# Moving the Mamba half of an output projection into the recurrent rounds before it

## The chip, the cores and the metric

One core of a Trainium2 chip runs the whole program. The metric is the device time of one execution in microseconds (us). TensorE multiplies, VectorE and ScalarE read its results from PSUM (eight banks of 512 float32 columns per partition), GpSimd and SyncE help with masks and transfers. A float32 product appears in the trace as two matmul records and two weight loads.

## The reference, cut to what matters

One inference step of a hybrid trunk with one layer. 384 tokens (128 of a prompt, 256 of a sample; three tiles of 128) with 1024 channels pass a modulated norm and an input projection. Two groups of heads work side by side. The Mamba group gives `ym` (384 x 1024). The RWKV group gives `yr` (384 x 1024), from a recurrence with a matrix state per head in two directions. Then

```
mix = jnp.concatenate([ym, yr], axis=-1) @ w_out        # w_out: 2048 x 1024
x = x + (gate1 * mix).astype(x.dtype)
h = rmsnorm(x, norm2_w) * (1.0 + scale2) + shift2
x = x + (gate2 * hierarchical_moe(h, ...)).astype(x.dtype)
```

The gates are row vectors, one for the prompt and one for the sample. The product with `w_out` is a sum of two halves: `ym` with the first 1024 rows of `w_out`, and `yr` with the last 1024.

## The kernel before, in words

The stages follow one another: modulation and input projection (to 350 us), the Mamba group (to about 468 us), the RWKV group (to 904 us), the out projection (904 to 995 us), norm and router (to 1029 us) and sixteen pairs of experts with their overflow (to the end). The order of instructions on every engine is written out by hand, and engines wait for each other by semaphores that count.

`mixm` holds `ym` with channels on partitions, eight tiles of 128 x 384, from the end of the Mamba group on. The RWKV group works through eight pairs of heads, one in each round (`round_pe`, `round_act`, `round_dve`, with c from 0 to 7; round 1 is c = 0). Its results take the place of tiles 0 to 7 of `um_a`.

A round has this order on TensorE. First come the small gram products (L485, L492) and one pair of larger ones (L513). Then four levels invert triangular blocks of 32 x 32: `blocks_32` (L531) multiplies 16 blocks for each of three units, ScalarE copies each unit (L754), `blocks_32` multiplies again, and VectorE merges (L930) and transposes (L933). One more group of gram products lies in each level. Then come pair products and half inverses (L544 to L563), the joining products (L616, L624), and the right sides, solutions `u`, states and outputs `y_out` (L637 to L688) for the units.

Between them `fill` puts twelve small products of the round before and of the round to come. Their numbers are MEAN, VAR (group norm of the pair before), KSQ (squared keys, L440), W_UP and W_UP + 1, A_UP and A_UP + 1 (decays and rates, two directions, each with 64 rows, L445), V_T (transpose), G_UP (L453), BE_T and KAP_T (four transposes each, L457) and BONUS. `aux_bank` puts even numbers in PSUM bank 6 and odd ones in bank 7, and `aux_free` lets a product start when the product two before it has been read:

```
def aux_bank(n, width):
    return ps[:, 6 + n % 2, 0:width]
...
pe.wait_ge(aux_act, c * 10 + (10 + n - 2))
```

ScalarE reads BE_T and KAP_T (L722, L724) at the very end of its round, behind `u_copy(2)` (L789). Before that come the exponentials, `y_copy(0)`, `rhs_copy(2)` and `y_copy(1)`.

SyncE's queue in the rounds holds only three loads of 64 KB a round, the next up projections. Once round 7 has released the space it loads 2 MB of `w_out`, and after the last round 6 MB more into the ring (`ring_a`), and the input `x` again.

The out projection (L1756 to L1777) has four blocks of four rows of tiles, 24 products of 512 columns each: two blocks with `mixm` and two with `um_a`. All sum up in PSUM banks 0 to 5 (three tiles, two halves of 512 columns). `gate_rows` (L1113) spreads a gate vector over the partitions in banks 6 and 7, and ScalarE copies it (L1999). VectorE then multiplies each tile of the product by the gate and adds it to `x` (L2313, L2315) in `x1_tile`.

Of the kernel before, what the change touches and what calls it, by code (L numbers as in the profile page):

```python
# [102 lines left out]
def program(nc, a, out):  # L103
    ctx = ExitStack()
    with ctx:
# [94 lines left out]
        us = [at(r, 3840, 2, 2, 64) for r in ring_s]  # L200
        sg = at(misc, 0, 2, T)
# [42 lines left out]
        vec_t = sem("vectors_transposed")  # L244
# [6 lines left out]
        cond_T = sem("conditions_transposed")  # L251
        ident_ok = sem("identity_ready")
        sel32_ok = sem("selector_ready")
# [144 lines left out]
        def aux_bank(n, width):  # L398
            return ps[:, 6 + n % 2, 0:width]

        def aux_free(pe, c, n):

            if n == MEAN:
                pe.wait_ge(aux_act, c * 10 + 10)
            elif n == VAR:
                pe.wait_ge(aux_dve, c * 2 + 2)
            elif n == KSQ:
# [3 lines left out]
            return aux_bank(n, T)  # L411
# [23 lines left out]
        def prep_pe(pe, c, n):  # L435
# [18 lines left out]
            elif n < BONUS:  # L454
                pe.wait_ge(ab_ok, c * 2 + (n - BE_T + 3))
                for i, (d, j) in enumerate(UNITS):
                    mm = pe.transpose(aux_bank(n, 4 * P)[:, P * i:P * i + P], (be, kap)[n - BE_T][:, d, j, :], ident[:, :])  # L457
# [108 lines left out]

        def round_pe(pe, c, b, prev, nxt):
# [132 lines left out]
            y_out(1)  # L700
            u(2)
            fill(BE_T, KAP_T)
# [3 lines left out]
        def prep_act(act, c, b, n):  # L706

            aux_there(act, c, n)
            src = aux_bank(n, T)
# [11 lines left out]
            elif n == BE_T:  # L721
                ins = act.activation(btks[b].rearrange("p i t -> p (i t)"), aux_bank(n, 4 * P), ACT.Copy)  # L722
            else:
                ins = act.activation(ktks[b].rearrange("p i t -> p (i t)"), aux_bank(n, 4 * P), ACT.Copy)  # L724
# [18 lines left out]
        def tail_act(act, c, n):  # L743
            aux_there(act, c, n)
            act.activation(ysq_c, aux_bank(n, T), ACT.Ln, scale=1.0 / 64, bias=eps_gn[:, 0:1]).then_inc(aux_act, 1)

        def round_act(act, c, b, prev, nxt):
# [3 lines left out]
            for l in range(1, 5):  # L751
# [3 lines left out]
                if l == 1:  # L755
                    if prev:
                        tail_act(act, c, VAR)
                    if nxt:
                        prep_act(act, c, 1 - b, KSQ)
                elif l == 2:  # L760
                    inverse_roots(act, c, prev, nxt)
                if nxt and l in (2, 3):
                    for n in ((W_UP, W_UP + 1) if l == 2 else (A_UP, A_UP + 1)):
# [72 lines left out]
        def prep_dve(dve, c, b, lc, part):  # L836
# [27 lines left out]
            else:  # L864
# [10 lines left out]
                dve.tensor_tensor(vbs[b], aux_bank(BONUS, T), v_c, ALU.mult).then_inc(aux_dve, 1)  # L875

        def tail_dve(dve, c, n, p, b, lc, part):

            if part == 0:
                aux_there(dve, c, n)  # L880
                dve.scalar_tensor_tensor(yc0, aux_bank(n, T), -1.0 / 64, y_c, ALU.mult, ALU.add).then_inc(aux_dve, 1)
# [214 lines left out]
        def wout_block(q):  # L1096

            if q == 0:
                return at(um_f, 8 * T, 4, D)
            return ring[:, q - 1].rearrange("p k c -> p (k c)").rearrange("p (k c) -> p k c", k=4)  # L1100

        def wout_ready(eng, q):
            if q == 0:
                eng.wait_ge(wout0_in, 16)
            else:
                eng.wait_ge(w_in_slot[q - 1], 16 * (N_BLOCKS // RING + 1))
# [150 lines left out]
        def _(sp):  # L1257
# [34 lines left out]
            with sp.Fori(0, 7) as c:  # L1292
                sp.wait_ge(aux_ps, c * 12 + 9)
                for i, w in enumerate(ups):
                    sp.dma_start(stw[:, i, :], w[:, ds(c * P + P, P)]).then_inc(up_loaded, 16)

            w_out_q = [a["w_out"][0, BLK * q:BLK * (q + 1)].rearrange("(k p) c -> p k c", p=P) for q in range(4)]
            sp.wait_ge(v_ok, 8)
            sp.wait_ge(ab_ok, 16)
            sp.dma_start(wout_block(0), w_out_q[0]).then_inc(wout0_in, 16)  # L1300
            sp.wait_ge(yo_rd, 27)
            x_row = [(x1[:, 0, :], a["x_prompt"][0]),
                     (x1[:, 1:3, :], a["x_sample"][0].rearrange("(j p) c -> p j c", p=P))]
            for q in range(1, 4):
                sp.dma_start(wout_block(q), w_out_q[q]).then_inc(w_in_slot[q - 1], 16)
# [7 lines left out]
            sp.wait_ge(out_ps, 6)  # L1313
# [48 lines left out]
        def _(pool):  # L1362
# [6 lines left out]
            pool.nop().then_inc(ident_ok, 1)  # L1369
# [37 lines left out]
            pool.wait_ge(vec_t, 1)  # L1407
# [86 lines left out]
        def _(pe):  # L1494
            pe.wait_ge(ident_ok, 1)
            pe.wait_ge(s_cond, 32)
            pe.transpose(ps[:, 0, 0:16], crows[:, :], ident[0:16, 0:16]).then_inc(cond_T, 1)
# [26 lines left out]
            pe.wait_ge(sel32_ok, 1)  # L1524
# [231 lines left out]
            for q in range(4):  # L1756
                if q == 1:
                    pe.wait_ge(pair_ok, 9)
                if q:
                    gate_rows(pe, q - 1)  # L1760
                if q == 3:
                    gate_rows(pe, 3)
                wout_ready(pe, q)
                w = wout_block(q)

                steps = ([(k, j) for k in range(4) for j in range(NTILE)] if q < 3 else
                         [(k, j) for j in range(NTILE) for k in range(4)])
# [713 lines left out]
```

## Time and profile before

| what | us |
|---|---|
| median of 3 runs | 1341.92 (1341.85 to 1343.03) |
| profiled execution, its own time | 1345.54 |
| its span, first to last instruction | 1343.8 |
| TensorE matmul busy in the span | 1178.0 (88%) |
| mean granted TensorE clock | 0.916 |
| rounds 2 to 7 | 545 to 848 |
| out projection | 904 to 995 |

Times in the rows are us from the start of the span. A busy time of TensorE means that matmuls were in flight; ends of matmuls are modelled. The granted clock is 1.0 at 2.4 GHz and 0.5 at 1.2 GHz. "issue" stands for time in which an engine waited for nothing that the profile shows.

### The profile page before, as it was taken

What the parts mean: (1) busy time and instruction counts of PE and PEld (TensorE: products, weight loads), DVE (VectorE), ACT (ScalarE), POOL (GpSimd) and SP (SyncE); (2) the same over time, 40 slices, a digit from 0 to 9 for tenths busy, and PEclk for the clock granted to TensorE, in tenths of its full rate; (3) what the DMA queues carried; (4) which work ended last, traced back from release to release, by engine and by line L of the source; (5) the groups of instructions that cost most, each with busy time, mean ns of one, the idle gap of its engine ahead of it and who ended that gap; (6) DMA issues with size and microseconds to landing.
All of it is one profiled execution on the core that took longest, in us unless ns stands there. A gap on an engine that the chain in (4) does not pass through costs nothing.

```text
span 1343.8 us, 35314 instructions
## 1 busy us (share of the span) xinstructions
PE 1178.0 (88%) x15632; PEld 780.4 (58%) x15632; DVE 576.5 (43%) x1366; ACT 336.6 (25%) x696; POOL 138.3 (10%) x186
## 2 busy tenths in 40 slices
PE   5898899999767878898888898889999999999991
PEld 4554356555566656676676676674556555555541
DVE  1354004445587565665665665530045222222214
ACT  2122011111212654444444544330012000000012
POOL 6000000000131033112022022000000000000002
PEclk9899998999877997887887987889999999999996
DMA  9436553146200000000000000115027799999974
GB/s 337 158 127 220 199 184 143 66 132 71 73 12 0 1 8 9 4 9 10 4 10 10 4 10 4 66 63 190 0 92 305 305 416 416 415 416 416 380 298 156
DMA packets 77774, 192.83 MB, mean 144 GB/s; under 512 B 11716, under 2 KB 26311, under 8 KB 73031
## 3 DMA queue, kind: packets, MB, share of 16 engines
q1 hardware_dynamic: 73504, 178.58, 36.5%
q10 hardware_dynamic: 3271, 9.08, 1.7%
q0 software_dynamic: 864, 3.15, 0.7%
q8 instruction: 113, 1.85, 0.6%
q14 instruction: 22, 0.18, 0.0%
HBM read 175.58 MB, written 15.20 MB: 142 GB/s over the span
## 4 chain that ended last, share of the span: by engine, by line
PE 78%; DVE 8%; issue 7%; ACT 3%; DMA 3%; POOL 0%; DVEq 0%; POOLq 0%; SPq 0%; ACTq 0%
PE ps L1547 15%; PE ps L1158 9%; PE ps L1147 7%; PE ps L1772 6%; PE ps L1178 5%; PE ps L531 4%; PE ps L1590 3%; PE ps L563 2%; PE ps L513 1%; DVE misc L2233 1%; DMA ring_a<-in_w_in 1%; PE ps L416 1%; PE ps L521 1%; PE ps L1509 1%; PE ps L637 1%
## 5 line engine op out<-in xcount | busy, mean ns | idle before, releaser
L1547 PE MATMUL ps<-hT,ring_a 128*128 128x384 f32 x624 | 208.3, 496 | 2.5 <-DVE hT L2087 2.5
L1547 PEld LDWEIGHTS ps<-hT,ring_a 128*128 128x128 f32 x624 | 120.2, 194 | 86.4 <-issue 5.9
L531 PE MATMUL ps<-ring_a 32*32 32x32 f32 x6144 | 74.7, 200 | 38.2 <-issue 38.1
L1147 PE MATMUL ps<-scratch,misc 128*128 128x128 f32 x864 | 99.7, 276 | 1.3 <-DVE scratch L1194 1.3
L1147 PEld LDWEIGHTS ps<-scratch,misc 128*128 128x128 f32 x864 | 97.9, 192 | 3.1 <-issue 3.1
L531 PEld LDWEIGHTS ps<-ring_a 32*32 32x32 f32 x6144 | 66.5, 112 | 56.8 <-issue 50.8
L2165 DVE SCALAR_TENSOR_TENSOR um_a<-ps,mum,um_a 128x127 f32 (+3 forms) x162 | 67.3, 416 | 71.2 <-ACT um_a L1919 42.4
L1158 PE MATMUL ps<-ring_a,um_a 128*64 128x512 f32 x288 | 63.4, 593 | 1.4 <-DVE um_a L1201 1.4
L1416 POOL TENSOR_TENSOR hT<-tri,la 128x512 f32<-128x512 f32 x24 | 25.4, 1087 | 365.6 <-PEq L1624 327.0
L1213 DVE COPY um_a<-ps 128x256 f32<-128x256 f32 x17 | 7.2, 424 | 125.5 <-PE ps L1167 125.5
L1158 PE MATMUL ps<-misc,um_a 128*64 128x512 f32 x128 | 56.3, 593 | 1.4 <-DVE um_a L1201 1.4
L1225 ACT ACTIVATE um_a<-ps 128x1024 f32<-128x1024 f32 x17 | 17.4, 1023 | 143.0 <-PE ps L1178 143.0
L1590 PE MATMUL ps<-ring_a,hT 128*128 128x512 f32 x96 | 46.8, 648 | 7.0 <-DMA ring_a<-in_w_in 7.0
L1201 DVE COPY um_a<-ps 128x1024 f32<-128x1024 f32 x17 | 20.8, 1224 | 71.4 <-PE ps L1147 70.7
L416 PE MATMUL ps<-ident 128*128 128x128 f32 x362 | 46.1, 289 | 1.6 <-DVE mixm L2286 1.6
L1488 POOL DMA_INDIRECT um_a<-expert_rows,wdt x6 | 6.7, 1121 | 395.9 <-DMA expert_rows<-um_a 390.0
L416 PEld LDWEIGHTS ps<-ident 128*128 128x128 f32 x362 | 45.4, 206 | 3.5 <-issue 2.9
L1158 PEld LDWEIGHTS ps<-ring_a,um_a 128*64 128x64 f32 x288 | 21.4, 137 | 41.3 <-issue 41.3
L930 DVE COPY_PREDICATED ring_a<-lvl,ps 128x128 f32<-128x128 int32 x96 | 26.8, 279 | 40.6 <-PE ps L531 40.5
L1772 PE MATMUL ps<-ring_a,um_a 128*128 128x512 f32 x96 | 41.5, 593 | 0.0
L1919 ACT ACTIVATE um_a<-ps,mum 128x384 f32 x24 | 13.9, 580 | 110.1 <-PE ps L1547 110.1
L2233 DVE SCALAR_TENSOR_TENSOR misc<-misc,dt,ring_a 128x128 f32<-128x128 f32 x96 | 36.0, 445 | 8.8 <-ACT misc L1943 8.8
(419 smaller groups left out, 2031.1 us busy)
## 6 DMA issues: line engine op xcount, KB each, us to landing
ring_a<-in_w_ada SPq DMA_DIRECT2D x12, 2048.0 KB, 12.6
ring_a<-in_w_in SPq DMA_DIRECT2D x11, 2048.0 KB, 9.3
ring_a<-in_moe_w_gate SPq DMA_DIRECT2D x18, 1024.0 KB, 9.6
ring_a<-in_moe_w_up SPq DMA_DIRECT2D x18, 1024.0 KB, 11.7
ring_a<-in_moe_w_down SPq DMA_DIRECT2D x18, 1024.0 KB, 11.7
expert_rows<-um_a ACTq DMA_DIRECT2D x17, 512.0 KB, 7.1
misc<-in_moe_w_gate SPq DMA_DIRECT2D x16, 512.0 KB, 9.3
misc<-in_moe_w_up SPq DMA_DIRECT2D x16, 512.0 KB, 11.8
```

The lines of the kernel that those rows point to most:

```text
L416: pe.matmul(place, ident[:, :], ident[:, :], start=True, stop=True)
L531: mm = pe.matmul(ps[r, 2 * s + 1, m:m + 32], lhs[r, h, d, :], rhs[r, h, d, :], start=True, stop=True, tile_position=(32 * q, 32 * q), skip ...
L563: mm = pe.matmul(ps[z, 2 * s + q % 2, o:o + 32], merge_of(s, d, h)[r], xcT[s][r, h, d, :], start=True, stop=True, tile_position=(32 * q, 6 ...
L930: dve.copy_predicated(xc[s], level_mask(l, False), ps[:, 2 * s + 1, P:2 * P].rearrange("p (h d q) -> p h d q", h=2, d=2)).then_inc(x_ok, 1)
L1147: mm = pe.matmul(ps[:, k // 4, P * (k % 4):P * (k % 4) + P], h2[:, j, P * k:P * k + P], pick[:, j, :], start=(j == 0), stop=(j == NTILE - 1))
L1158: mm = pe.matmul(ps[h, 2 + b, :], xgT[:, b, k, h], gate_up_tile(b, x, k), start=(k == 0), stop=(k == KT - 1), tile_position=(0, CH * x), s ...
L1178: mm = pe.matmul(ps[h, 5 + c, :], hidT[:, b, k, h], wdn[b][x][:, k, BLK * c:BLK * c + BLK], start=(k == 0), stop=(k == 1), tile_position=( ...
L1547: mm = pe.matmul(ps[:, t % 4 if isinstance(t, int) else t, 0:T], slot(n)[:, k, P * c:P * c + P], hT[:, k, :], start=(k == 0), stop=(k == K ...
L1590: mm = pe.matmul(ps[:, i % 4, :], hT[:, k, P * j:P * j + P], slot(n)[:, k, :], start=(k == 0), stop=(k == KT - 1))
L1772: mm = pe.matmul(ps[:, 2 * j + c, :], src[:, P * j:P * j + P], w[:, k, BLK * c:BLK * c + BLK], start=(kk_ == 0), stop=(kk_ == 15))
L2165: step(dve.scalar_tensor_tensor(dst, src, mus(m), dst, ALU.mult, ALU.add), i)
L2233: ins = dve.scalar_tensor_tensor(seg[:, j, 4 * d + h, :], seg[:, j, 4 * d + h, :], dt[:, j, ds(grp * 8 + (16 * d + 4 * q + h), 1)], msc[:, ...
```

## The change

The 48 products of the Mamba half are computed in rounds 2 to 7 (c from 1 to 6), eight in each: one behind the first and one behind the second group of level products of each of the four levels (`mamba_out`). A round makes one block of the half product, one tile of 128 tokens by 512 columns, and accumulates it in PSUM bank 7 over the eight channel tiles. ScalarE copies the finished block to SBUF (`half_mix`) behind V_T. For this bank 7 is taken from the small products: in the rounds all of them use bank 6, and each waits until the one before it has been read. W_UP and W_UP + 1, and A_UP and A_UP + 1, which stood together, are put in different places of the levels, KSQ moves from level 1 to level 2, and BE_T moves ahead of `u(2)`.

The weights come in 48 loads of 256 KB on SyncE's queue, three ahead, into free columns of the three ring slots. Behind the rounds only the RWKV half is left: 48 products, with the four gate products in between. Its weights come in four loads, three of them during the last rounds. VectorE multiplies the six blocks by the gate and adds them to `x` (twelve operations of 128 x 512) before `x1_tile(0)`. Three semaphores at the start are merged into others.

```diff
+        mamba_w = [at(r, 3072, BLK) for r in ring_s]
+        half_mix = [at(um_flat, (8 * T, 16 * T)[r // 3] + BLK * (r % 3), BLK) for r in range(6)]
...
-        def aux_bank(n, width):
-            return ps[:, 6 + n % 2, 0:width]
+        def aux_bank(c, n, width):
+            return ps[:, 6 + n % 2 if c < 0 or (c == 7 and n >= KSQ) else 6, 0:width]
...
-                pe.wait_ge(aux_act, c * 10 + (10 + n - 2))
+                pe.wait_ge(aux_act, c * 10 + (10 + n - 1))
...
+        def mamba_out(pe, c, k):
+
+            if not 1 <= c <= 6:
+                return
+            r, n = c - 1, 8 * (c - 1) + k
+            if k == 0 and r:
+                pe.wait_ge(half_rd, r)
+            mamba_block(pe, n)
+            pe.matmul(ps[:, 7, :], mixm[:, k, P * (r // 2):P * (r // 2) + P], mamba_w[n % RING],
+                      start=(k == 0), stop=(k == KT - 1)).then_inc(half_ps, 1)
...
                     blocks_32(pe, s, 0, diag(s), xc[s]).then_inc(yl_ps, 1)
+                mamba_out(pe, c, 2 * l - 2)
+                if l > 1:
+                    fill({2: KSQ, 3: W_UP + 1, 4: A_UP + 1}[l])
                 if l == 4:
                     gram_pair(pe, c, arr, 4)
...
                     blocks_32(pe, s, P, xcT[s], yc[s]).then_inc(zl_ps, 1)
-                if l > 1:
-                    fill(*{2: (W_UP, W_UP + 1), 3: (A_UP, A_UP + 1), 4: ()}[l])
+                mamba_out(pe, c, 2 * l - 1)
+                if l in (2, 3):
+                    fill({2: W_UP, 3: A_UP}[l])
                 if l < 4:
                     gram_pair(pe, c, arr, l)
                 if l == 1:
-                    fill(VAR, KSQ)
+                    fill(VAR)
...
             y_out(1)
+            fill(BE_T)
             u(2)
-            fill(BE_T, KAP_T)
+            fill(KAP_T)
             y_out(2)
             fill(BONUS)
...
                 prep_act(act, c, 1 - b, V_T)
+            if 1 <= c <= 6:
+                act.wait_ge(half_ps, 8 * c)
+                act.activation(half_mix[c - 1], ps[:, 7, :], ACT.Copy).then_inc(half_rd, 1)
...
+            def mamba_weights(n):
+
+                if n >= RING:
+                    sp.wait_ge(half_ps, n - RING + 1)
+                r, k = n // KT, n % KT
+                sp.dma_start(mamba_w[n % RING], a["w_out"][0, P * k:P * k + P, BLK * (r % 2):BLK * (r % 2) + BLK]
+                             ).then_inc(w_in_slot[n % RING], 16)
...
-            for q in range(4):
...
+            steps = [(k, j) for k in range(4) for j in range(NTILE)] + [(k, j) for j in range(NTILE) for k in range(4, 8)]
+            for k, j in steps:
+                if j == 0:
+                    wout_ready(pe, k)
+                    if 3 <= k < 7:
+                        if k == 3:
+                            pe.wait_ge(pair_ok, 9)
+                        gate_rows(pe, k - 3)
+                for c in range(2):
+                    mm = pe.matmul(ps[:, 2 * j + c, :], um_a[:, k, P * j:P * j + P], wout_tile(k)[:, BLK * c:BLK * c + BLK],
+                                   start=(k == 0), stop=(k == KT - 1))
+                if k == KT - 1:
                     mm.then_inc(out_ps, 1)
...
+            for r in range(6):
+                j, c = r // 2, slice(BLK * (r % 2), BLK * (r % 2) + BLK)
+                dve.tensor_tensor(half_mix[r], half_mix[r], g1[:, min(j, 1), c], ALU.mult).then_inc(half_w, 1)
+            for r in range(6):
+                j, c = r // 2, slice(BLK * (r % 2), BLK * (r % 2) + BLK)
+                dve.wait_ge(half_w, r + 1)
+                dve.tensor_tensor(x1[:, j, c], x1[:, j, c], half_mix[r], ALU.add).then_inc(half_w, 1)
+            dve.wait_ge(half_w, 12)
             x1_tile(0)
```

## Rows read from the trace of the kernel before

**Rows 1.** Chain that ended last, 900 to 1000 us: start, us, what

```profile
904.12 20.87 PE ps L1772 x48
924.98 1.78 PE ps L1113 x16
926.77 20.60 PE ps L1772 x48
...
971.58 1.03 ACT misc L1999
...
995.31 4.80 PE ps L416 x43
```

**Rows 2.** Windows of rounds 2 to 7 and of the out projection

```profile
core 0: us, PE busy (x) PEld busy (x) DVE busy (x) ACT busy (x) POOL busy (x), PEclk, DMA share, GB/s
545.00:848.00 303.00, 263.52 (x8492) 206.50 (x8490) 189.82 (x460) 137.45 (x339) 60.38 (x59) 0.85 0.03 7
904.00:995.30 91.30, 90.07 (x258) 44.03 (x259) 7.52 (x9) 9.43 (x14) 0.54 (x4) 1.00 0.22 84
```

**Rows 3.** Waits of TensorE, 545 to 848 us: total, times, longest

```profile
PE ps L531 <- issue: 25.7, 19, 2.5
...
PE ps L440 <- DVE misc L841: 1.3, 4, 0.4
```

**Rows 4.** Windows of the level parts of rounds 2 to 7, TensorE alone

```profile
599.00:621.00 22.00, 17.48 (x856) 0.88 0.02 4
...
sum 132.00, PE 104.71; mean PE 17.45
```

**Rows 5.** Order of TensorE's work in the levels of one round

```profile
598.27 0.91 PE L468 MATMUL ps<-hT,bones 128*128 128x384 f32 x2
599.12 2.23 PE L531 MATMUL ps<-ring_a 32*32 32x32 f32 x192
601.27 1.14 PE L513 MATMUL ps<-misc 64*128 64x256 f32 x8
...
608.31 0.27 PE L531 MATMUL ps<-ring_a 32*32 32x32 f32 x9 [2.11 <-issue]
608.50 1.33 PE L445 MATMUL ps<-um_a,stw 64*128 64x384 f32 x4
609.62 1.93 PE L513 MATMUL ps<-misc 64*128 64x256 f32 x8
...
613.67 0.92 PE L445 MATMUL ps<-um_a,stw 64*128 64x384 f32 x4
614.42 1.06 PE L521 MATMUL ps<-misc 64*128 64x128 f32 x16
```

**Rows 6.** DMA view, 599 to 625 us in 40 slices

```profile
GB/s 0 0 0 0 0 25 0 0 0 0 25 0 0 0 0 0 25 0 0 0 0 0 0 25 0 0 0 0 25 0 0 0 0 0 38 0 0 0 0 25
...
q8 instruction: 7, 0.11, 1.9%
```

**Rows 7.** Windows around one stretch of half clock: PE busy, clock, DMA

```profile
599.10:608.90 9.80, 7.34 (x399) 1.00 0.01 3
608.90:612.30 3.40, 3.40 (x76) 0.50 0.02 5
...
619.10:632.80 13.70, 11.91 (x321) 0.50 0.07 18
```

**Rows 8.** Chain that ended last: packed products of 384 columns

```profile
69.28 5.16 PE ps L1547 x16
```

**Rows 9.** Order of work at the end of a round

```profile
641.97 1.09 PE L457 MATMUL ps<-ident,misc 128*128 128x128 f32 x8
...
642.34 0.38 ACT L789 ACTIVATE ring_a<-ps 128x256 f32<-128x256 f32 x1
642.66 0.60 ACT L722 ACTIVATE scratch<-ps 128x512 f32<-128x512 f32 x1
643.00 0.66 PE L678 MATMUL ps<-ring_a,misc 128*64 128x128 f32 x8
```

**Rows 10.** VectorE, products and sums of 128x512

```profile
L2276 DVE TENSOR_TENSOR misc<-misc,ring_a x8: 691/691/691, 439.0 to 450.4; 128x512 f32<-128x512 f32 x8
```

**Rows 11.** DMA issues: KB each, us to landing

```profile
um_a<-in_w_out SPq DMA_DIRECT2D x1, 2048.0 KB, 7.8
```

More of the change, by code:

```diff
@@ L754, in round_act @@
                     act.activation(yc[s].rearrange("p h d c -> p (h d c)"), ps[:, 2 * s + 1, 0:P], ACT.Copy).then_inc(yl_ok, 1)
-                if l == 1:
-                    if prev:
-                        tail_act(act, c, VAR)
+                if l == 1 and prev:
+                    tail_act(act, c, VAR)
+                elif l == 2:
                     if nxt:
                         prep_act(act, c, 1 - b, KSQ)
-                elif l == 2:
                     inverse_roots(act, c, prev, nxt)
-                if nxt and l in (2, 3):
-                    for n in ((W_UP, W_UP + 1) if l == 2 else (A_UP, A_UP + 1)):
+                if nxt and l > 1:
+                    for n in ((), (W_UP,), (W_UP + 1, A_UP), (A_UP + 1,))[l - 1]:
                         prep_act(act, c, 1 - b, n)
@@ L1094, in program, with wout_ready, wout_tile @@
         y_ok = sem("y_ready")
[L1096 to L1106, printed above, removed]
+        WOUT = [(at(mx_f, 0, 3, D), 0, 3), (at(um_f, 12 * T, 1, D), 3, 1), (at(um_f, 20 * T, 2, D), 4, 2),
+                (at(ring_a, 0, 2, D), 6, 2)]
+        wout_in = [wout0_in] + w_in_slot
+        def wout_ready(eng, k):
+            for i, (v, k0, n) in enumerate(WOUT):
+                if k == k0 + n - 1 or k == k0:
+                    eng.wait_ge(wout_in[i], 16 if i == 0 else 16 * (N_BLOCKS // RING + 16 + 1))
+        def wout_tile(k):
+            return next(v[:, k - k0] for v, k0, n in WOUT if k0 <= k < k0 + n)
         def gate_rows(pe, m):
@@ L1291, in _ @@
                 sp.dma_start(stw[:, i, :], w[:, 0:P]).then_inc(up_loaded, 16)
[L1292 removed]
+            def mamba_weights(n):
[4 more added lines that the diff above has]
+                             ).then_inc(w_in_slot[n % RING], 16)
+            sp.wait_ge(proj, XBC + 6 + RT)
+            sp.wait_ge(off_ps, 8)
+            sp.wait_ge(wkv_T, 1)
+            sp.wait_ge(out_done, 32)
+            for n in range(RING):
+                mamba_weights(n)
+            for c in range(7):
+                for n in range(8 * c - 13, 8 * c - 5):
+                    if n >= RING:
+                        mamba_weights(n)
                 sp.wait_ge(aux_ps, c * 12 + 9)
                 for i, w in enumerate(ups):
[L1295 to L1297 removed]
+                    sp.dma_start(stw[:, i, :], w[:, c * P + P:c * P + 2 * P]).then_inc(up_loaded, 16)
+            for n in range(6 * KT - 5, 6 * KT):
+                mamba_weights(n)
+            sp.wait_ge(half_ps, 6 * KT)
             sp.wait_ge(v_ok, 8)
             sp.wait_ge(ab_ok, 16)
[L1300 to L1301 removed]
+            sp.wait_ge(aux_ps, 7 * 12 + 9)
+            for i, (v, k, n) in enumerate(WOUT):
+                if i == 3:
+                    sp.wait_ge(yo_rd, 27)
+                sp.dma_start(v, a["w_out"][0, D + P * k:D + P * (k + n)].rearrange("(k p) c -> p k c", p=P)).then_inc(wout_in[i], 16)
             x_row = [(x1[:, 0, :], a["x_prompt"][0]),
                      (x1[:, 1:3, :], a["x_sample"][0].rearrange("(j p) c -> p j c", p=P))]
[L1304 to L1305 removed]
             for dst, src in x_row:
@@ L1755, in _ @@
             pe.wait_ge(gcol_ok, 1)
-            for q in range(4):
[L1757 to L1767, printed above, removed]
-                for k, j in steps:
-                    kk_ = 4 * q + k
-                    src = mixm[:, kk_, :] if kk_ < 8 else um_a[:, kk_ - 8, :]
-                    for c in range(2):
-                        mm = pe.matmul(ps[:, 2 * j + c, :], src[:, P * j:P * j + P], w[:, k, BLK * c:BLK * c + BLK],
-                                       start=(kk_ == 0), stop=(kk_ == 15))
-                    if q == 3 and k == 3:
-                        mm.then_inc(out_ps, 1)
-                if q < 3:
+            steps = [(k, j) for k in range(4) for j in range(NTILE)] + [(k, j) for j in range(NTILE) for k in range(4, 8)]
[10 more added lines that the diff above has]
+                if k == KT - 1:
                     mm.then_inc(out_ps, 1)
@@ L2449, in y_tile @@
                                          ALU.mult).then_inc(y_ok, 1)
+            dve.wait_ge(gate_ok, 4)
             x2_tile(0)
```

60 lines of the change are left out of this document (33 added, 27 removed).

## The prediction

> **What bounds the kernel now.** I read the chain of work that ended last first, because it says whose time counts. At the end of the eight rounds it is TensorE alone [rows 1]: the out projection stands on it as four blocks with the gate products between them, and the next stage starts right behind at 995.31. The windows say the same [rows 2]: TensorE is busy for 90.07 of 91.30 us there, at full clock, while VectorE and ScalarE have under 10 us of work. So what leaves this stretch shortens the kernel in full.
>
> The rounds are less plain. In rounds 2 to 7 (545 to 848 us) TensorE is busy for 263.52 of 303.00 us at a mean clock of 0.85 [rows 2]. That leaves 39.5 us idle, 6.6 us a round. The list of waits puts it down to "issue" before the small level products (25.7 us in 19 pauses), and only 1.3 us to VectorE [rows 3]. Most of it lies in the level part: six windows of 22 us there hold 104.71 us of work in 132, so 4.5 us idle each [rows 4].
>
> What is "issue" here? The order of TensorE's work shows a pause of 2.11 us inside one run of identical 32x32 products, ending at 608.31 [rows 5]; a wait for another engine would stand before a product that needs something new. The DMA view of 599 to 625 us shows what moves meanwhile: almost nothing but the instruction queue, seven packets of 16 KB, in slices of 0.65 us number 5, 10, 16, 23, 28, 34 and 39, so one every 3.7 us [rows 6]. The packet of slice 10 begins at 605.5 and TensorE goes on at 608.31; the one of slice 16 starts 1.1 us after that. TensorE uses 856 matmul records and as many weight loads in 22 us [rows 4], about 290 a packet. I read the pauses as hunger for instructions: a run of 192 level records (and 192 loads) is over in 2.15 us, faster than a packet comes. Work that takes long per instruction costs little in such a stretch, and this is what the change brings.
>
> A pause costs twice. After the one that ends at 608.31 the granted clock is half (1.2 GHz) from 608.9 to 612.3 and full (2.4 GHz) around it [rows 7]. In it the pair of decay products shows 1.33 us against 0.92, and four gram products 1.93 against 1.14 [rows 5]: 1.2 us lost, and each of the six level parts has such a stretch of 3.4 us or more (their mean clock is 0.84 to 0.94).
>
> **The sum, part by part.** *Removed behind the rounds:* 48 products of 512 columns, 96 records, which take 20.87 and 20.60 us [rows 1]: 41.5. The last two gate products stood back to back and the second waited 1.1 us for ScalarE's 1.03 us copy; now two products of 0.86 us lie between them: 1.1 more. Together 42.6 us.
>
> *Added in rounds 2 to 7:* eight products a round. Packed, one takes 20.60/24 = 0.86 us. Alone between small ones it costs more: the mean product (384 columns) holds the engine from 598.27 to 599.12, 0.85 us [rows 5], while the same width packed takes 5.16/8 = 0.645 [rows 8]. I add these 0.2 us: 1.06 each, 8.5 us a round, with 6.9 as the lower bound. The Trainium skill ("TensorEngine Tiling (Array Packing)", Key Properties) says that a change of tiling mode drains TensorE, which speaks against putting full products between 32x32 ones; by it the sum takes 8.5, without such a cost 6.9, and the row sides with it.
>
> *Moved small products.* Today the two decay products, 64 rows each, run as a pair in other halves of the array: from 613.67 to 614.42, 0.75 us for both [rows 5]. The change splits them, and the two rate products too, with level products between; alone each costs about the 0.85 of the mean product. 2 x (2 x 0.85 - 0.75) = 1.9 us a round. The squares product moves from level 1 to level 2, where its input is long ready (its 0.2 us wait goes).
>
> *One bank for the small products.* Each waits until the one before it is read. In the levels ScalarE reads between two of them while TensorE has over 1 us of other work, so nothing. At the round's end it bites: the second transpose needs the first one read, but ScalarE reads it only behind the copy of u(2). Today u(2) ends, the eight transposes run from 641.97, and y_out(2) starts at 643.00 [rows 9]. Then the first four transposes come before u(2), so u(2) ends near 642.5; ScalarE copies u (0.38) and the first transpose (0.60), overlapping slightly, until 643.5; four transposes follow and y_out(2) starts near 644.0. That is 1.0 us in each of rounds 1 to 7 (between 0.5, if ScalarE is quicker to start, and 1.4).
>
> *At nothing:* ScalarE's copy of the finished 128x512 block, 0.60 us by the same shape [rows 9], lies where it waits for the half inverses. VectorE's twelve 128x512 operations at 0.69 us [rows 10], 8.3 us, start when the second gate is copied, near 25.4 us into the new out projection, and end at 33.7; the first tile of the product is ready at 34.6 (32 products of 0.86, 4 gates of 1.8). If they were late, tile 0's scaling would be, and the last tile comes only 13.7 us later. The 256 KB weight loads on SP: 2048 KB land in 7.8 us [rows 11], and a load is issued three products, some 8 us, ahead. SP's queue then holds the next up projections behind them, which stay a round ahead as now. The semaphores that are merged at the start add no instruction.
>
> *What the pauses give back.* Added TensorE time per round: 8.5 + 1.9 + 1.0 = 11.4 us. Where a packet's instructions last longer than 3.7 us, no pause is left. The level part's own work is about 22 - 4.5 - 1.2 = 16.3 us; with 10.4 more it is 26.7, against 22 us that the packets need today, and the new products are spread one to each half level. So I take 5.8 of the 6.6 us of idle as filled (a remainder before the half inverses stays) and the 1.2 us of half clock as won back: 11.4 - 5.8 - 1.2 = 4.4 us a round, 26.4 in six. Round 1 has no new product; 1.9 + 1.0 less what its pauses swallow: 1.0. Net: -42.6 + 26.4 + 1.0 = -15.2 us. The profiled execution took 1345.54 us with a span of 1343.8; the median of the runs shown is 1341.92, and from it I come to **1327 us** (rounded).
>
> **The rivals.** *Nearly free.* A product costs 0.86, all 6.6 us fill, and the half clock behind the levels (0.50 from 619.1 to 632.8 [rows 7]) gives back another 0.8: 11.4 - 1.6 - 6.6 - 1.2 - 0.8 = 1.2 us a round, 7.2 - 42.6: 1306. For it: little there but TensorE and packets. Against: the drain row.
>
> *The pauses are not filled, slower.* If they are dependences or a fixed fetch cost that moves along, the full 11.4 x 6 + 2.9 = 71.3 stands against 42.6: 1371; with half of the 7.8 us of idle and half clock recovered, 7.5 a round, about 1347. It decides once a round grows by 6.9 us, that is when less than 4.5 us is recovered. Against it: pauses inside runs of equal products. The Trainium skill ("Runtime: NRT & Kernel Launch", Instruction fetch mechanics) says fetches come in 16 KiB blocks of 256 instructions and are mostly hidden; by that the pauses are something else, and this rival's 1371 is the time. The packet size agrees with the trace, hidden does not.
>
> *Weight loads hold up the instruction packets.* Eight loads of 256 KB a round share the DMA engines with some seven packets. If each packet were late by as long as one load lasts at the rate of rows 11 (7.8/8, 1.0 us), the packets would need 22 + 7 = 29 us for 26.7 of work: 2.3 us a round more, 1341, no change. It tips to slower from 1.3 us a packet.
>
> **How the numbers follow.** The likeliest, 0.53, has its own range of 1314 to 1338 (product 0.86 to 1.1, 4.5 to 6.6 us filled). Nearly free 0.19, pauses not filled 0.19, loads in the way 0.09. 0.2% (2.7 us) is about what a measurement of this kernel can tell from no change. Faster takes the first two and a little of the mild forms of the others: 0.75; same 0.07; slower 0.18. The range reaches from the free case's 1306 (less 1 for its rounding) to 1345, short of the half-filled case's 1347, and leaves 0.1 on either side.
>
> **What would show it.** The out projection's stretch shrinks from 91.2 to about 48.6 us. Rounds 2 to 7 grow from about 50.4 to 54.7 us, the pauses inside the level products nearly vanish, the level parts run at clock 1.00, packets stay about one every 3.7 us or sparser, and a new wait on ScalarE's transpose copy stands before the second four transposes. The prediction is wrong if a round grows by over 6 or under 2.5 us, if TensorE waits for a weight load, or if the products show double time.

## The result and the profile after

| | median us (lowest to highest) | ratio to before |
|---|---|---|
| before, same chip | 1342.01 (1341.85 to 1343.03) | 1 |
| after, 4 runs | 1309.2 (1306.97 to 1313.71) | 0.9758 [0.9732, 0.9785] |

The kernel is 32.8 us faster. The forecast was 1327 us, a gain of about 15 us: the sign is right and the time lies in the range, but the size of the gain is not right. The profiled execution of after took 1313.71 us, 31.8 us less than that of before.

The first view is that of the windows, rounds 2 to 7 and the out projection, where the answers to [rows 2] stand. The columns are those of that group.

```profile
541.20:862.50 321.30, 303.14 (x8719) 209.70 (x8718) 200.26 (x469) 144.37 (x348) 65.62 (x60) 0.96 0.16 47
915.20:963.80 48.60, 48.59 (x162) 25.62 (x163) 14.84 (x21) 9.36 (x13) 0.54 (x4) 1.00 0.14 47
```

The same stretch of before, from the start of its second round to that of its eighth, TensorE alone:

```profile
542.50:849.28 306.78, 267.30 (x8623) 0.86 0.03 9
```

The out projection shrank from 91.2 to 48.6 us. Six rounds grew by 14.5 us, 2.4 us a round. The prediction had named less than 2.5 us as a sign that it is wrong. The rest is small: before round 1 -2.7, round 1 +1.4 (50.8 to 52.2), round 8 -2.1 (54.8 to 52.7), behind the out projection -0.4. The sum is -31.9.

Look at what happened inside the six rounds. TensorE's busy time rose by 35.8 us and its idle time fell from 39.5 to 18.2. Yet the 48 products at 1.06 us (50.9) and the split pairs (8.9, measured below) are 59.8 us of work. So 24.0 us of busy time vanished: instructions took less time than before. The granted clock tells why. It rose from 0.86 to 0.96, and from this mean the time at half clock is (1 - 0.86) x 2 x 306.8 = 86 us before, and 26 us after. So 60 us less at half clock go with 24.0 us less of busy time, 0.40 us for each. The two variants `e11` and `f2` in the table below, with nearly the same work, give the same price: 39 us more at half clock, 16.2 us more busy, 0.42 for each.

The list of TensorE's waits, 541.2 to 862.5 us, answers to [rows 3]:

```profile
PE ps L537 <- issue: 4.3, 4, 1.7
PE ps L662 <- DVE ring_a L987: 3.1, 3, 1.5
PE ps L463 <- ACT misc L748: 2.9, 3, 1.0
PE ps L463 <- ACT scratch L748: 2.9, 3, 1.0
PE ps L569 <- issue: 2.3, 3, 1.3
```

The pauses before level products (L537, L531 before) fell from 25.7 to 4.3 us. The new wait for ScalarE before the second transposes (L463) is there in all six rounds, 0.97 us each. VectorE now holds up L662 for 3.1 us.

The order of TensorE's work in the levels of one round, as in [rows 5]:

```profile
600.40 1.12 PE L585 MATMUL ps<-ring_a,mixm 128*128 128x512 f32 x2
601.46 1.05 PE L537 MATMUL ps<-ring_a 32*32 32x32 f32 x96
602.43 1.13 PE L585 MATMUL ps<-ring_a,mixm 128*128 128x512 f32 x2
603.49 1.14 PE L519 MATMUL ps<-misc 64*128 64x256 f32 x8
...
614.11 0.91 PE L451 MATMUL ps<-um_a,stw 64*128 64x384 f32 x2
614.95 1.06 PE L537 MATMUL ps<-ring_a 32*32 32x32 f32 x96
```

A Mamba product (L585) holds TensorE from 600.40 to 601.46, so 1.06 us; a decay product alone (L451) takes 0.84. No pause is left in this stretch. The windows of three level parts, as in [rows 4], show that it is not so in every round:

```profile
599.00:621.00 22.00, 21.95 (x733) 1.00 0.26 75
651.00:673.00 22.00, 20.31 (x618) 0.92 0.21 64
706.00:728.00 22.00, 21.38 (x729) 1.00 0.25 75
```

The DMA view of 599 to 625 us, as in [rows 6]:

```profile
q8 instruction: 6, 0.10, 1.6%
...
ring_a<-in_w_out SPq DMA_DIRECT2D x8, 256.0 KB, 2.8
```

Six packets came where seven came before: TensorE now needs fewer instructions a microsecond (733 matmul records in the first 22 us above, 856 in [rows 4]). A weight load lands in 2.8 us, and TensorE never waits for one.

The end of a round, order of work, as in [rows 9]:

```profile
644.25 0.38 ACT L817 ACTIVATE ring_a<-ps 128x256 f32<-128x256 f32 x1 [0.38 <-PE ps L678]
644.52 0.59 ACT L748 ACTIVATE scratch<-ps 128x512 f32<-128x512 f32 x1
645.17 0.66 PE L463 MATMUL ps<-ident,misc 128*128 128x128 f32 x4 [0.97 <-ACT scratch L748]
645.76 0.66 PE L703 MATMUL ps<-ring_a,misc 128*64 128x128 f32 x8
```

ScalarE copies `u(2)`, then the first transpose, and only then may the four others use the bank. `y_out(2)` (L703) comes behind them.

In the out projection VectorE's twelve operations (L2362, L2366) end before the first tile of the product is ready for L2351 (order of VectorE's work):

```profile
940.82 3.70 DVE L2362 TENSOR_TENSOR um_a<-um_a,misc 128x512 f32<-128x512 f32 x6 [22.60 <-ACT misc L2037]
944.44 3.69 DVE L2366 TENSOR_TENSOR misc<-misc,um_a 128x512 f32<-128x512 f32 x6
950.21 1.23 DVE L2351 TENSOR_TENSOR misc<-ps,misc 128x1024 f32<-128x1024 f32 x1 [2.07 <-PE ps L1812]
```

### The profile page after: what moved, and what is told of

Same layout as the page of the kernel before. It is cut to its first block, busy times and chain, and to the rows that moved or that the text cites. A ratio compares the mean times of both kernels' runs of the same rounds, so it can differ in the third digit from the quotient of the medians.

```text
span 1311.9 us, 35341 instructions
## 1 busy us (share of the span) xinstructions
PE 1170.4 (89%) x15632; PEld 761.3 (58%) x15632; DVE 592.1 (45%) x1378; ACT 342.6 (26%) x702; POOL 142.9 (11%) x186
## 4 chain that ended last, share of the span: by engine, by line
PE 80%; DVE 8%; issue 4%; ACT 4%; DMA 3%; POOL 0%; DVEq 0%; POOLq 0%; SPq 0%; ACTq 0%
PE ps L1594 16%; PE ps L1186 9%; PE ps L1175 7%; PE ps L537 5%; PE ps L1206 5%; PE ps L585 4%; PE ps L1637 4%; PE ps L1812 3%; PE ps L519 2%; PE ps L451 1%; DVE misc L2271 1%; DMA ring_a<-in_w_in 1%; PE ps L422 1%; PE ps L527 1%; PE ps L662 1%
## 5 line engine op out<-in xcount | busy, mean ns | idle before, releaser
L537 PEld LDWEIGHTS ps<-ring_a 32*32 32x32 f32 x6144 | 63.6, 108 | 41.1 <-issue 28.8
L537 PE MATMUL ps<-ring_a 32*32 32x32 f32 x6144 | 72.1, 197 | 13.5 <-issue 13.4
L1463 POOL TENSOR_TENSOR hT<-tri,la 128x512 f32<-128x512 f32 x24 | 25.4, 1088 | 363.1 <-PEq L1671 324.7
L585 PE MATMUL ps<-ring_a,mixm 128*128 128x512 f32 x96 | 54.7, 652 | 0.0
L1957 ACT ACTIVATE um_a<-ps,mum 128x384 f32 x24 | 13.9, 580 | 109.8 <-PE ps L1594 109.8
```

The costliest lines, as they stand in the source:

```text
L537: mm = pe.matmul(ps[r, 2 * s + 1, m:m + 32], lhs[r, h, d, :], rhs[r, h, d, :], start=True, stop=True, tile_position=(32 * q, 32 * q), skip ...
L585: pe.matmul(ps[:, 7, :], mixm[:, k, P * (r // 2):P * (r // 2) + P], mamba_w[n % RING], start=(k == 0), stop=(k == KT - 1)).then_inc(half_p ...
```

## The experiments

Each run stands beside runs of before on its chip, whose medians lay between 1342.68 and 1344.96 us. "Rounds" is the length of rounds 2 to 7 in the profile of the run, then TensorE's busy time and mean granted clock in them. The out projection took 48.6 us in every variant of after. TensorE's idle time in the rounds is their length less its busy time.

| kernel | median, ratio | rounds, busy, clock |
|---|---|---|
| before | | 306.8, 267.3, 0.86 |
| after | 1309.2, 0.9758 | 321.3, 303.1, 0.96 |
| after again (`f1`) | 1307.99, 0.9727 [0.9704, 0.975] | 312.8, 295.8, 0.98 |
| `e2` before, more level products | 1380.8, 1.0255 [1.0217, 1.0293] | 334.0, 284.2, 0.84 |
| `e3` after, more level products | 1332.36, 0.9909 [0.9879, 0.9938] | 327.1, 307.2, 0.97 |
| `e5` before, pairs split | 1340.3, 0.9991 [0.9958, 1.0024] | 309.7, 276.2, 0.86 |
| `f4` before, code shifted | 1339.03, 0.997 [0.995, 0.9989] | 307.7, 265.9, 0.86 |
| `e12` after, code shifted | 1306.64, 0.9731 [0.9687, 0.9775] | 316.7, 300.5, 0.97 |
| `e6` two banks at the round's end | 1295.95, 0.9695 [0.9637, 0.9753] | 307.4, 293.5, 0.99 |
| `f2` the same again | 1298.41, 0.9664 [0.9637, 0.9691] | 305.5, 292.9, 0.99 |
| `e7` products doubled | 1341.71, 1.0007 [0.9979, 1.0035] | 344.9, 332.6, 1.00 |
| `e8` products in pairs | 1308.81, 0.9766 [0.9728, 0.9805] | 318.1, 292.9, 0.98 |
| `e10` two banks and pairs | 1303.36, 0.9706 [0.967, 0.9742] | 314.6, 294.6, 0.97 |
| `e11` two banks, last product later | 1308.61, 0.9732 [0.9695, 0.9768] | 320.1, 309.1, 0.93 |
| `f3` products in rounds 1 and 8 | 1310.37, 0.9752 [0.9726, 0.9777] | 315.2, 295.6, 0.98 |
| `e1` products 8 wide | left-out part, see below | 328.8, 300.4, 0.84 |
| `e9` products 256 wide | left-out part | 310.2, 287.1, 0.94 |
| `e4` three weight loads | left-out part | 315.5, 299.9, 0.97 |

One pair of rows rules how all others are read. After and `f1` are the same kernel, their medians agree, and yet the six rounds of their profiled executions differ by 8.5 us, 7.3 of them busy time, at clocks of 0.96 and 0.98. A difference of that size between two single profiles is no evidence.

### Is it the length of the products that brings the clock back?

`e1`: everything of the change stays (bank, waits, loads, instructions), but a product has 8 columns.

```diff
-            pe.matmul(ps[:, 7, :], mixm[...], mamba_w[n % RING],
+            pe.matmul(ps[:, 7, 0:8], mixm[...], mamba_w[n % RING][:, 0:8],
```

> The changed kernel, but each Mamba product in the rounds streams 8 columns of its weights instead of 512; weight loads, instructions and waits are the same. The mix lacks the rest of the Mamba half. Theory (TensorE starves for instructions in the levels, and the starving lowers its clock; long products fill both): shortening 48 products from 1.06 us to about 0.3 us, 36 us of work, returns the pauses and the half clock instead of time, so rounds 2 to 7 take about 52 us each instead of 53.6 and the kernel about 1300 us, with idle in the rounds near 6 us a round and the clock near 0.87. Rival (the products' time is simply added and the gain comes from elsewhere): about 1273 us.

The mix lacks nearly all of the Mamba half, so the experts get other tokens and their stage takes 394 us in place of 348. Only the rounds are compared. The windows of rounds 1, 2 to 7 and 8, TensorE alone, and two groups of waits:

```profile
487.87:538.63 50.76, 44.67 (x1435) 0.87 0.03 7
538.63:867.46 328.83, 300.40 (x8720) 0.84 0.16 46
867.46:922.09 54.63, 44.32 (x1434) 0.81 0.16 58
```

```profile
L585 PE MATMUL ps<-ring_a,mixm x96: 256/277/382, 543.4 to 841.3; 128*128 128x8 f32 x96
```

```profile
PE ps L537 <- issue: 15.7, 19, 2.0
```

A narrow product holds TensorE for 0.24 to 0.32 us in this trace, so 36 to 40 us less are to compute. Yet the six rounds are 7.5 us longer than after's and 16.0 longer than `f1`'s. The busy time is nearly that of after (300.4 against 303.1) because everything else lasted longer: the clock fell back to 0.84. The pauses came back too, 15.7 us against 4.3. That is more than the theory had expected: 54.8 us a round for its 52. So the full products pay for a large part of themselves, in both ways, and the clock is the larger.

Do the products raise the clock only because they fill the pauses? The prediction took that for granted ("A pause costs twice"). The table speaks against it. `e8`, with full products in pairs, is idle for 25.2 us in the six rounds, nearly as long as `e1` with 28.4, and its clock is 0.98:

```profile
535.49:853.62 318.13, 292.90 (x8720) 0.98 0.16 47
```

`e11` is idle for only 11.0 us and its clock is 0.93. So idle time does not order the clock. With one product in each place, 8 columns give 0.84, 256 give 0.94 and 512 give 0.96 and 0.98; two of 512 give 1.00 (`e9` and `e7`, below).

`e7` goes the other way: each product twice, and the copy halves the sum.

```diff
+            for rep in range(2):
+                mm = pe.matmul(..., start=(k == 0 and rep == 0), stop=(k == KT - 1 and rep == 1))
...
-  act.activation(half_mix[c - 1], ps[:, 7, :], ACT.Copy)
+  act.activation(half_mix[c - 1], ps[:, 7, :], ACT.Copy, scale=0.5)
```

> The changed kernel with each Mamba product done twice and the copy scaled by one half, so the output stays. One more product packed behind the first costs 0.86 us, 6.9 us a round, 41 us in six. Theory: with one product in each place the pauses in the levels are almost gone (2 us a round are left) and the clock is 0.96, so most of it now adds: rounds 2 to 7 take 58.5 to 60 us, total 1338 to 1348 us. Rival (TensorE has more room than the pauses show): below 1330 us.

```profile
543.60:888.52 344.92, 332.63 (x8816) 1.00 0.15 44
```

48 more products at the packed 0.86 us are 41 us. The rounds grew by 23.6 us against after's profile and 32.1 against `f1`'s, the whole kernel by 33 us. The total came as expected, the rounds (57.5 us each) 1 us shorter. With the clock at 1.00 little is left to win back, so a second set pays about four fifths of its price.

`e9`: the products have 256 columns, the other half is left out.

```diff
-            pe.matmul(ps[:, 7, :], mixm[...], mamba_w[n % RING],
+            pe.matmul(ps[:, 7, 0:256], mixm[...], mamba_w[n % RING][:, 0:256],
```

> The changed kernel with Mamba products of 256 columns instead of 512 (half of the Mamba mix is missing, so the stages behind the out projection are not compared). A product then holds TensorE about 0.63 us instead of 1.06: 20 us less work in rounds 2 to 7. Theory (the clock pays for the products): with 8 columns these rounds took 328.8 us at clock 0.84, with 512 they took 321.3 us at 0.96; 256 lies between in clock (0.88 to 0.94) and takes 315 to 328 us, not 301. Rival (the narrow run was a special case, the time follows the work): 301 us.

```profile
541.71:851.96 310.25, 287.14 (x8720) 0.94 0.17 49
```

The rounds took 310.2 us, shorter than the theory's 315 to 328 and longer than the rival's 301; the clock of 0.94 is the theory's. Width alone does not order the lengths (8: 328.8; 256: 310.2; 512: 312.8 and 321.3; twice 512: 344.9); only the ends of the series are further apart than one kernel's profiles are.

### Are the pauses hunger for instructions?

`e2` and `e3` put 64 more of the smallest products into each round of before and of after (the first unit's level products twice): 256 more instructions, about 1.4 us by the rate of [rows 5].

```diff
                 for s in range(3):
+                    if s == 0:
+                        blocks_32(pe, s, 0, diag(s), xc[s])
                     blocks_32(pe, s, 0, diag(s), xc[s]).then_inc(yl_ps, 1)
```

> The kernel before, with the level products of the first unit done twice in each of the four levels (the same blocks to the same place): 64 more 32x32 products a round, 256 more instructions. Theory of the instruction packets: one packet more a round, 3.7 us each, 29 us in eight rounds, so about 1371 us. Rival (the pauses have another cause, such as waits between engines): the products cost what their rows show, 2.15 us per 96 of them, 1.4 us a round, 11 us, so about 1353 us, or less if they fall into the pauses.

> The changed kernel with the same doubled level products. Theory of the instruction packets: in rounds 2 to 7 TensorE's own work now lasts about as long as the packets, so the extra packet costs less than on the kernel before there (2 to 3 us a round) and the full 3.7 us in rounds 1 and 8: about 1330 us. Rival: 1.4 us a round as on the kernel before, about 1320 us.

Waits of `e2` in its rounds 2 to 7, then of `e3`:

```profile
PE ps L531 <- issue: 39.4, 25, 2.7
```

```profile
PE ps L537 <- issue: 5.1, 10, 1.1
```

In before the rounds grew by 27.2 us, 4.5 a round, three times the work and more than the 3.7 of the theory; the total is 1380.8 where 1371 was expected. The pauses at L531 grew by 13.7 us, all idle time by 10.3, and the busy time by 16.9, twice what 1.4 us a round makes, at a clock of 0.84. In after they grew by 5.8 us (14.3 against `f1`), 1.0 to 2.4 a round. In rounds 1 and 8 of `e3`, where no Mamba product lies, they cost 5.0 and 5.3 us (6.3 and 3.7 against `f1`), and its total of 1332.36 is the theory's. Small instructions are dear where they come in long runs and cheap where long products lie between.

The traces say it more directly. Rounds 2 to 7 of before, then of `e2`, in the DMA view:

```profile
q8 instruction: 68, 1.11, 1.6%
```

```profile
q8 instruction: 74, 1.21, 1.5%
```

`e2` has 256 more instructions a round and six more packets in six rounds. And when each pause ends can be set beside the start of the last packet of this queue. In before all 27 "issue" pauses in these rounds (36.6 us) end 2.2 to 2.8 us after a packet started, although packets start 3.3 to 8.8 us apart; in after all ten that are left end 2.2 to 2.9 us after one. After's waits for ScalarE and VectorE end anywhere from 0.6 to 7.6 us after one. The pauses are a lack of instructions, and a dependence would not show this.

`f3` puts eight products of 256 columns, used by nobody, into rounds 1 and 8 of after.

```diff
             if not 1 <= c <= 6:
+                pe.wait_ge(w_in_slot[0], 16 * (N_BLOCKS // RING + 1))
+                pe.matmul(ps[:, 7, 0:256], ident[:, :], mamba_w[0][:, 0:256], start=True, stop=True)
                 return
```

> The changed kernel with eight more products in each of rounds 1 and 8, where it has none: 256 columns by the identity, at the places that the Mamba products have in the other rounds, results unused. By rows of this case one holds TensorE 0.63 us, so 5.0 us of work a round. Theory (long products fill the pauses and raise the clock): rounds 1 and 8 take the same time or less (52 and 53 us, within 2 us each) at a clock of 0.94 or more instead of 0.84 to 0.87. Rival (work adds): each takes 5 us more.

```profile
488.86:538.83 49.97, 45.64 (x1450) 0.97 0.03 8
...
854.00:908.34 54.34, 46.33 (x1450) 0.91 0.16 58
```

Round 1 took 50.0 us (50.9 in `f1`), round 8 took 54.3 (54.3). The clock rose from 0.87 to 0.97 in round 1. In round 8 it rose from 0.84 to 0.91, less than the 0.94 expected, and hardly above the 0.90 that `e7` has there without any product. In round 1, with 5.0 us of work added, the busy time rose by 0.9. The added work cost nothing that can be measured.

### Do the weight loads or the split pairs cost?

`e4` makes only the first three of the 48 weight loads; the other products use stale weights.

```diff
-                for n in range(8 * c - 13, 8 * c - 5):
-                    if n >= RING:
-                        mamba_weights(n)
...
-            for n in range(6 * KT - 5, 6 * KT):
-                mamba_weights(n)
```

> The changed kernel with only the first three of the 48 weight loads; all products use those three pieces (so the mix is wrong). If the loads delay the instruction packets, the rounds get shorter without them, by up to 2.3 us each, 14 us in all (about 1296 us). If they do not, 1307 to 1311 us.

Its rounds took 315.5 us, between the 312.8 and 321.3 of the kernel with all loads. The loads cost nothing that shows.

`e5` is before with only the new order of the small products (pairs split, KSQ in level 2), and both banks.

```diff
+                if l > 1:
+                    fill({2: KSQ, 3: W_UP + 1, 4: A_UP + 1}[l])
...
-                    fill(*{2: (W_UP, W_UP + 1), 3: (A_UP, A_UP + 1), 4: ()}[l])
+                if l in (2, 3):
+                    fill({2: W_UP, 3: A_UP}[l])
```

> The kernel before with only the order of the small products changed (the squares product in level 2, the decay and rate pairs split and placed as in the changed kernel), in two banks as before. No Mamba product moves. The prediction's term: 1.9 us more TensorE work a round. Theory (pauses swallow it): rounds 1 to 7 longer by less than 1 us each, total 1342 to 1347 us. Rival (it adds): 13 us more, about 1357 us.

The busy time rose by 8.9 us in six rounds, 1.5 a round against 1.9 forecast. The rounds grew by 2.9 us and the total did not change (0.9991): even this small work filled pauses.

### What does the single bank cost?

`e6`, and `f2` again beside `f1`: KAP_T goes to bank 7, which is free at the round's end, and both transposes stand behind `u(2)` as before.

```diff
-            return ps[:, 6 + n % 2 if c < 0 or (c == 7 and n >= KSQ) else 6, 0:width]
+            return ps[:, 6 + n % 2 if c < 0 or (c == 7 and n >= KSQ) else 7 if n == KAP_T else 6, 0:width]
...
+            elif n == KAP_T:
+                if c:
+                    pe.wait_ge(half_rd, c)
...
-            if k == 0 and r:
-                pe.wait_ge(half_rd, r)
+            if k == 0:
+                pe.wait_ge(aux_act, c * 10 + 10)
...
-            fill(BE_T)
             u(2)
-            fill(KAP_T)
+            fill(BE_T, KAP_T)
```

> The changed kernel, but the second four transposes go to bank 7 (free by then) and both fours stand behind u(2) as before, so that they no longer wait for ScalarE. The prediction's term is 1.0 us in each of rounds 1 to 7. Theory: this wait lies where packets come in time, nothing fills it, so it comes back in full: 7 us less, about 1303 us. Rival (it is swallowed like the rest): no change, 1309 us.

> The kernel of e6 unchanged. The waits it removes are 6.8 us long in the trace of the changed kernel. If only they come back, 7 us below f1; if the 13 us of e6 were real, 13 us below f1; e10 and e11, which hold the same edit, came out 6 and 1 us below the changed kernel, so I expect 5 to 13 us below f1.

> The changed kernel unchanged, on the same chip as the three others of this call: 1306 to 1313 us.

The windows of `f2`, rounds 1 and 2 to 7, and of `f1`:

```profile
492.03:540.44 48.41, 41.62 (x1433) 0.93 0.03 8
540.44:845.92 305.48, 292.89 (x8719) 0.99 0.16 48
```

```profile
493.47:544.33 50.86, 44.70 (x1435) 0.87 0.03 7
544.33:857.12 312.79, 295.79 (x8720) 0.98 0.16 48
```

`e6` came to 1295.95, below both of its expectations, and `f2` lies in its range. The wait before L463 is gone, and the intervals of the two ratios do not meet: 1298.41 against 1307.99, 9.6 us. The waits were 5.8 us in rounds 2 to 7 and 1.0 in round 1. About 3 us more came with them. In these two profiles they are busy time (round 1 lost 3.1 us of it, at 0.93 instead of 0.87), but `e4` and `e8` show 0.93 in round 1 without this edit, so how they came is not settled. This is the best version.

### Where the products stand

`e8` has two products behind the second group of each level, `e10` adds the two banks, and `e11` is `e6` with the eighth product moved to the half inverses.

```diff
-                mamba_out(pe, c, 2 * l - 2)
...
+                mamba_out(pe, c, 2 * l - 2)
                 mamba_out(pe, c, 2 * l - 1)
```

```diff
-                mamba_out(pe, c, 2 * l - 1)
+                if l < 4:
+                    mamba_out(pe, c, 2 * l - 1)
...
                 half_inverses(pe, s)
+                if s == 0:
+                    mamba_out(pe, c, 7)
```

> The changed kernel with the eight products of a round in four places instead of eight (two behind the second group of level products of each level). Four switches of tile shape fewer, 0.2 us each, 0.8 us a round, 5 us in all, if TensorE's own work sets the pace: about 1304 us. If the packets do (evenness matters), pauses come back before the second group: 1309 to 1318 us. I expect the second, about 1312 us.

> The changed kernel with both edits: second transposes in bank 7, and the products in pairs behind the second level group. The first alone gave 1296 us, the second alone left 1309. Expected 1296 us, between 1290 and 1302; if the clock is now always high, the saved switches (5 us) show and it is nearer 1291.

> The changed kernel with the second transposes in bank 7 and the eighth product of a round moved from level 4 into the half inverses, behind the first unit, where pauses of about 1 us a round are left; the copy of the block stands behind the three unit copies. Theory: the product fills this pause instead of standing where none is left, up to 1 us a round: about 1291 us. Rival: the units behind it wait for it, 1296 to 1302 us.

The largest groups of waits in rounds 2 to 7 of `e8`, then of `e11`:

```profile
PE ps L537 <- issue: 13.9, 14, 2.1
```

```profile
PE ps L542 <- issue: 3.1, 6, 1.3
```

In pairs, longer runs of level products go hungry again: 13.9 us in 14 pauses against 4.3. Fewer changes between tile shapes would cost less busy time, and it is 292.9 us against `f1`'s 295.8, too little for single profiles to show. `e8` equals after in time. `e10` missed its range of 1290 to 1302 us: 1303.36. It is 5 us below `e8`, and their intervals meet, so in this arrangement the second bank gives back less, and how much is not clear. `e11` missed its expectation: 1308.61, no better than after and worse than `e6`. Its busy time is 309.1 at a clock of 0.93. Its largest group of pauses holds 3.1 us, no more than `f2`'s 3.5, so the loss is not pauses. Its rounds show what the clock costs; the fastest and the slowest of the six:

```profile
750.50:800.00 49.50, 48.29 (x1454) 1.00 0.18 51
800.00:855.63 55.63, 54.10 (x1454) 0.88 0.12 36
```

Why the clock fell is not shown.

### Does the place of the code matter?

`e12` and `f4` put 32 identity products (128 instructions, half a packet) at the program's start, in after and in before.

```diff
+            keep_warm(pe, ps[:, 3, 0:P], 32)
```

> The changed kernel with 32 more identity products (128 instructions, half a packet) at the start, where TensorE waits for its first weights. Nothing in the rounds changes but the place of the packet borders. If the pauses hang on where borders fall in a round, single rounds change by 1 to 3 us and the total by up to 8 us either way (1301 to 1317 us); if the pauses have nothing to do with packets, every round keeps its length within what repeated runs differ by, and the total is 1309 us.

> The kernel before with 32 more identity products (half a packet) in the wait for the first weights. Only the packet borders move. The kernel before is all pauses, so single rounds may change by 1 to 3 us, the total by up to 6 us either way around 1343; without any part of the packets, no round changes.

```profile
537.51:854.21 316.70, 300.46 (x8720) 0.97 0.16 48
```

After is unchanged by it, and before came out 4.4 us faster with more instructions to run. The six rounds of `f4`'s profile are not shorter (307.7 against 306.8), so the place of the packets in them is not shown to be the cause; that the added products change something at the start of the kernel is a rival that no run separates. Either way a shift of the code is worth a few us at most, and the gain of 33 us is far beyond that.

## Why the prediction was right in sign and wrong in size

- **Behind the rounds: right.** Forecast 42.6 us, measured 42.6 (91.2 to 48.6). VectorE's twelve operations were expected from 25.4 to 33.7 us into the stretch and ran from 25.6 to 32.9.
- **The added work: right.** A product took 1.06 us as forecast; the rival with the packed 0.86 was wrong there. The rule of the Trainium skill ("TensorEngine Tiling (Array Packing)", Key Properties) that a change of tiling mode drains TensorE agrees with these 0.2 us. The split pairs cost 1.5 a round for 1.9. The wait for the single bank came to 0.97 for 1.0.
- **The pauses: nearly right.** Forecast was that 5.8 of 6.6 us a round fill. The "issue" pauses in the list fell from some 36.6 to 8.7 us, 4.7 a round. With the new wait TensorE's idle time fell by 3.55 a round where the sum had 4.8. `e2`, `e3` and the ends of the pauses 2.2 to 2.9 us behind a packet's start bear out the reading as hunger for instructions. The Trainium skill ("Runtime: NRT & Kernel Launch", Instruction fetch mechanics) calls the cost of crossing from one 16 KiB block to the next mostly hidden; the 27 pauses of 36.6 us contradict it for such code.
- **"the 1.2 us of half clock won back": this step failed.** That half clock would be won back was right, and its size was not. It gave back 4.0 us a round in after's profile (24.0 / 6). I had priced the one stretch inside the levels [rows 7], and left the longer one behind them, 13.7 us at half clock, to the rival with 0.8 us. In fact the half clock fell from about 86 to 26 us in six rounds, behind the levels too. The forecast missed by 17.6 us. In rounds 2 to 7 these 2.8 us a round are 16.8 of them; the added work, 0.43 a round too high, gives 2.6 more, and the idle time, 1.25 a round too hopeful, takes 7.5 back: 11.9. The other 5.7 are round 8, the start, and the 1.0 us between the difference of the profiled executions and that of the medians. `e1` is the proof that the clock hangs on the long products: take away their columns alone, and it is 0.84 again. The prediction's reason, that the pauses bring the half clock and filling them ends it, does not hold as it stands: `e8` has nearly the idle time of `e1` at a clock of 0.98. The sum tied the clock to the pauses in the levels and so left out the stretch behind them. The exact split between clock and pauses is not settled, since busy time holds both slow clock and other slowness; `f1`'s profile would give (59.8 - 28.5) / 6 = 5.2 us a round.
- **The rivals.** "Nearly free" (1306) came nearest in time, with another account: the product was dearer, fewer pauses filled, and far more clock came back than its 2.0 us. "Pauses not filled" is refuted by the waits. "Weight loads hold up the packets" is refuted by `e4` and by 2.8 us to landing. (Its tipping point was mis-added: by its own terms the kernel is clearly slower from 1.1 us a packet on, not 1.3.)

What stays open: the order of the rounds' lengths in the width series, what two banks save beyond the waits and why less of it came in `e10` and `e11`, the clock of `e11`, and the 2 to 3 us before round 1 and in round 8, which are no larger than one kernel's profiles differ by.

## What to carry to other kernels

Where TensorE runs many tiny products and the trace shows "issue" pauses between equal ones, long products from a later stage can be put between them for about a quarter of their packed time (here 42.6 us left the tail, 32.8 were gained, so 9.8 were paid for 41.5). Singly they left fewer pauses than in pairs, but the time was the same. Price every stretch at half clock in the round, not only the one where the new work lies. And when such a move takes a PSUM bank, look first for the point in the round where that bank is idle: giving it back there was worth 10 us here, though less in two other arrangements.

## What the hardware showed that was not expected

- More work gave TensorE a higher clock: 48 products of 512 columns raised the mean granted clock of six rounds from 0.86 to 0.96 and 0.98, twice as many to 1.00, and the same 48 at 8 columns left it at 0.84. Eight of 256 columns raised a round from 0.87 to 0.97 at no cost in time.
- Idle time does not order the clock: 28.4 us idle at 0.84 (`e1`), 25.2 at 0.98 (`e8`), 11.0 at 0.93 (`e11`).
- Every "issue" pause of TensorE in rounds 2 to 7, before and after, ended 2.2 to 2.9 us after an instruction packet began to move.
- 256 more instructions of the smallest kind cost 4.5 us a round without long products beside them and 1.0 to 2.4 with them.
- One kernel's six rounds differ by 8.5 us between two profiled executions (321.3 and 312.8) while the medians of its runs agree within 1.2 us.
